# Two hybrid attention layers on one Trainium2 core: first logits, latent values, 1/sum and the start of the output projection in another order

## The reference, cut to what matters

```python
def hybrid_layer(x, ...):
    h = rms_norm(x, g_norm)
    z = jnp.einsum('bsd,dc->bsc', h, w_in)
    aq, ak, av, ag, bq, bk, bv, bg, cq, ckv, ckr, cg = jnp.split(z, idx, axis=-1)
    # A: 6 heads, keys and values shared by 3; rms norm, axial rope, full softmax
    oa = dense_gqa_blocks(qa, ka, va, HEAD_DIM ** -0.5) * jax.nn.silu(ag)
    # B: 6 heads, window of +-128 keys, a sink term in the sum
    ob = windowed_sink_gqa(qb, kb, vb, b_sink, HEAD_DIM ** -0.5) * jax.nn.silu(bg)
    # C: 4 heads, queries, keys and values out of latents cq and ckv
    qc = jnp.einsum('bsr,rc->bsc', rms_norm(cq, c_qn), c_wuq)
    kv = jnp.einsum('bsr,rc->bsc', rms_norm(ckv, c_kvn), c_wukv)
    oc = mla_blocks(qc_nope, qc_rope, kc_nope, kc_rope, vc, ...) * jax.nn.silu(cg)
    o = jnp.concatenate([oa, ob, oc], axis=-1)
    return x + jnp.einsum('bsm,md->bsd', o, w_out)
```

## Time and profile before

| | us |
|---|---|
| median of three executions | 1965.51 |
| lowest, highest | 1963.92, 1968.25 |
| the profiled execution: whole time | 1968.18 |
| the profiled execution: span of its instructions | 1966.4 |
| TensorE busy | 1878.5 (96%) |
| TensorE weight loads busy | 1489.7 (76%) |
| VectorE busy | 817.7 (42%) |
| ScalarE busy | 782.1 (40%) |
| GpSimd busy | 597.8 (30%) |

### The profile page before, as it was taken

How to read it: one execution, slowest core, us unless ns; L and a number is a source line. 1 busy time by engine, 2 the same in 40 slices (tenths; PEclk the granted TensorE clock), 3 DMA queues, 4 the chain that set the end, 5 groups by cost and what they waited for, 6 DMA issues and landing times.

```text
span 1966.4 us, 23067 instructions
## 1 busy us (share of the span) xinstructions
PE 1878.5 (96%) x9756; PEld 1489.7 (76%) x9756; DVE 817.7 (42%) x1338; ACT 782.1 (40%) x1286; POOL 597.8 (30%) x182
## 2 busy tenths in 40 slices
PE   8998899989999999999899999989998999998997
PEld 5777799988788888887788888877674468765456
DVE  7663545653123212102562035135635644625653
ACT  5974465443333333223332122224335533334541
POOL 3331432032232333444254434433420005322001
PEclk9998899989999999999899999989999999999999
DMA  5110000122323332232132323223110012211001
GB/s 198 65 65 0 1 1 21 45 91 75 135 96 107 97 112 85 87 107 86 45 127 86 107 86 107 86 86 137 67 65 22 1 43 99 86 63 44 1 1 43
DMA packets 28992, 141.54 MB, mean 72 GB/s; under 512 B 2871, under 2 KB 7351, under 8 KB 14936
## 3 DMA queue, kind: packets, MB, share of 16 engines
q1 hardware_dynamic: 18944, 122.94, 17.4%
q10 hardware_dynamic: 9944, 17.12, 2.6%
HBM read 134.80 MB, written 5.24 MB: 71 GB/s over the span
## 4 chain that ended last, share of the span: by engine, by line
PE 90%; DVE 4%; ACT 3%; POOL 2%; issue 1%; DMA 0%; POOLq 0%; SPq 0%; DVEq 0%; ACTq 0%
PE bank L403 54%; PE bank L1032 8%; PE bank L607 5%; PE bank L414 4%; PE bank L1977 3%; PE bank L1998 3%; PE bank L1984 2%; PE bank L1437 1%; ACT w_part L361 1%; PE bank L1413 1%; PE bank L655 1%; PE bank L1926 1%; PE bank L792 1%; ACT WK L2107 1%; PE bank L1068 1%
## 5 line engine op out<-in xcount | busy, mean ns | idle before, releaser
L403 PE MATMUL bank<-x_part,w_part 128*128 128x512 f32 x3264 | 764.8, 394 | 0.6 <-DVE x_part L571 0.6
L403 PEld LDWEIGHTS bank<-x_part,w_part 128*128 128x128 f32 x3264 | 614.6, 189 | 135.0 <-issue 6.1
L2424 POOL TENSOR_TENSOR w_part<-RAW,w_part 128x2048 fp32r<-128x2048 f32 (+1 forms) x90 | 402.9, 4480 | 819.4 <-ACT w_part L361 819.4
L2424 POOL TENSOR_TENSOR w_part<-WK,w_part 128x2048 fp32r<-128x2048 f32 (+1 forms) x30 | 125.1, 4169 | 376.7 <-ACT w_part L361 376.7
L361 ACT ACTIVATE w_part<-RAW 128x2048 fp32r<-128x2048 f32 (+1 forms) x90 | 166.5, 1851 | 175.7 <-PE bank L403 138.3
L403 PE MATMUL bank<-f_part,w_part 128*128 128x512 f32 x768 | 174.4, 389 | 0.0
L403 PEld LDWEIGHTS bank<-f_part,w_part 128*128 128x128 f32 x768 | 144.1, 188 | 29.9
L1032 PE MATMUL bank<-WK 128*128 128x128 f32 (+1 forms) x1056 | 125.0, 279 | 5.3 <-DVE WK L1265 3.7
L1032 PEld LDWEIGHTS bank<-WK 128*128 128x128 f32 (+1 forms) x1056 | 119.7, 194 | 7.6 <-DVE WK L1265 4.0
L1977 PE MATMUL bank<-WK 64*128 64x512 f32 (+3 forms) x256 | 81.7, 593 | 9.7 <-ACT STAT L2093 9.7
L903 DVE SCALAR_TENSOR_TENSOR WK<-bank,COL,WK 128x510 f32<-128x510 f32 (+1 forms) x96 | 71.6, 749 | 46.3 <-ACT WK L863 43.7
(11 more groups left out here) (281 smaller groups left out, 2392.8 us busy)
## 6 DMA issues: line engine op xcount, KB each, us to landing
RAW<-wts SPq DMA_DIRECT2D x84, 1024.0 KB, 4.8
WK<-wts SPq DMA_DIRECT2D x24, 1024.0 KB, 4.8
WK<-scratch ACTq DMA_DIRECT2D x16, 256.0 KB, 2.7
RAW<-wts SPq DMA_DIRECT2D x6, 512.0 KB, 3.4
WK<-wts SPq DMA_DIRECT2D x6, 512.0 KB, 3.5
scratch<-WK ACTq DMA_DIRECT2D x4, 768.0 KB, 3.3
WK<-xT SPq DMA_DIRECT2D x4, 512.0 KB, 5.8
WK<-xT ACTq DMA_DIRECT2D x1, 2048.0 KB, 12.7
```

The costliest lines, as they stand in the source:

```text
L403: mm = pe.eng.matmul(b[:, :], W[w][:, k, c:c + P], src[x][k], start=start and k == 0 and n == 0, stop=stop and k == kn - 1 and n == 2)
L2424: eng.tensor_tensor(low_part(i), raw_part(i), high_part(i).bitcast(F32), ALU.subtract).then_inc(w_split, 1)
```

## The change

In both layers:

- TensorE waits for `kready` (last key copy of ScalarE) and `qready` (last query rope of VectorE) instead of `ready` and `ready_act`. `gated` on VectorE now waits for its gate.
- Gates 0 to 3 get banks 0 to 3 in a pool of their own; the query rotations, gates 4 to 7 and the latent values get banks 4 to 7.
- The latent values (`uv`) are made in step 1 of the attention, and VectorE copies them instead of ScalarE.
- ScalarE's rounding for the last gate chunk moves from before the dummy Exp to step 6.
- GpSimd multiplies eight identities by the 1/sum columns of a head pair (`inverse_diagonal`), and TensorE spreads by two products of a block of ones with 512 columns of these scaled identities.
- `fm4` is cut in two functions; its banks come from the logits' pool, and k = 0 and 1 stand before the value products of the last head pair.

```diff
-        def fm(name, chunk, c0, src, bank=None, start=True, stop=True, need=None):
+        def fm(name, chunk, c0, src, bank=None, start=True, stop=True, need=None, pool=range(BANKS)):
...
-            b = bank if bank is not None else job(name)
+            b = bank if bank is not None else job(name, pool)
...
-        def fm4(names, chunk, src, need):
+        def fm4_banks(names, chunk, pool=range(BANKS)):
+            return [weights(chunk, c) for c in (0, 256)], [job(n, pool) for n in names]
+        def fm4_steps(names, halves, bs, src, need, ks):
             pe = q["pe"]
-            halves = [weights(chunk, c) for c in (0, 256)]
-            bs = [job(n) for n in names]
-            for k in range(len(src[0])):
+            for k in ks:
...
+        GATE_BANKS = (0, 1, 2, 3), (4, 5, 6, 7)
+        SPREAD = wk(35584, 2 * TT, P)
...
-                    fm((L, "G", j), f"L{l}G{g}", j % 4 * P, HTS)
+                    fm((L, "G", j), f"L{l}G{g}", j % 4 * P, HTS, pool=GATE_BANKS[g])
...
-            pe.wait_ge(*at((L, "ready")))
-            pe.wait_ge(*at((L, "ready_act")))
+            pe.wait_ge(*at((L, "kready")))
+            pe.wait_ge(*at((L, "qready")))
+            def late_values():
+                for t in range(TT):
+                    b = job((L, "uv", t), GATE_BANKS[1])
+                    E.matmul(b[:, 0:256], CL[:, 2, t * P:(t + 1) * P], UKV[:, 256:512], start=True, stop=True)...
...
-                pe.wait_ge(*at((L, "ri", m)))
-                for t in range(TT):
-                    for o in range(2):
-                        z = 80 + 4 * ((2 * m + o) % 4) + t
-                        mm = E.matmul(b[64 * o:64 * o + 64, t * P:(t + 1) * P], LST[:, z:z + 1].broadcast_to([P, 64]), ident, start=True, stop=True)
+                pe.wait_ge(*at((L, "ridiag", m)))
+                for o in range(2):
+                    mm = E.matmul(b[64 * o:64 * o + 64, :], ones[:, 0:64], SPREAD[:, TT * o:TT * o + TT, :], start=True, stop=True)
...
+                if i == 1:
+                    late_values()
+                if i == len(pairs) + 1:
+                    halves, bs = fm4_banks(outs, f"L{l}O0", LOGIT_BANKS)
+                    fm4_steps(outs, halves, bs, mixed, lambda k: (L, "mix", k), (0, 1))
...
-            fm4([(L, "O", i) for i in range(4)], f"L{l}O0", mixed, lambda k: (L, "mix", k))
+            fm4_steps(outs, halves, bs, mixed, lambda k: (L, "mix", k), range(2, KO))
             for i in range(4, KO):
                 fm((L, "O", i), f"L{l}O1", i % 4 * P, mixed)
...
-                    if j % 2:
+                    if j % 2 and j < KO - 1:
                         ahead(f"L{l}G{g}", (j - 1) % 4 * P)
...
+                if i == 6:
+                    ahead(f"L{l}G1", 2 * P)
...
+                if i == 1:
+                    for t in range(TT):
+                        dve.wait_ge(*at(("pe", (L, "uv", t))))
+                        V.tensor_copy(VT2[:, t, 256:512], ps((L, "uv", t))[:, 0:256])...
...
+            def inverse_diagonal(L, m):
+                pool.wait_ge(*at((L, "ri", m)))
+                if m:
+                    pool.wait_ge(*at(("pe", (L, "sp", m - 1))))
+                ri = LST[:, 80 + 8 * (m % 2):88 + 8 * (m % 2)]
+                eng.tensor_tensor(SPREAD, ident.unsqueeze(1).broadcast_to([P, 8, P]), ri.unsqueeze(2).broadcast_to([P, 8, P]), ALU.mult)...
```

42 lines of the change are left out of this document (27 added, 15 removed).

## The result

The changed kernel takes 1950.91 us (median of four executions, 1947.6 to 1951.27); the kernel before took 1965.29 in the same session (four, 1963.92 to 1968.25). The ratio is 0.9921, with a 95% interval of 0.9905 to 0.9938. The forecast was 1949.3, in a range of 1943 to 1956: right in sign, and 1.6 us off in size. The profiled execution spans 1949.1 us; the one of before spanned 1966.4.

What follows compares the result with a forecast made beforehand. TensorE, 90% of the span, was taken as the bound. Savings of 10.7 us in layer 0 and 11.1 in layer 1, less 5.6 lost, made 16.2 off the 1965.5 median: 1949.3 us, range 1943 to 1956.

Steps and rivals of the forecast that it cites:

- The bound: Whole kernel: TensorE is 90% of the span; changes off TensorE count only where TensorE waits for them.
- Part 1: Attention start, earliest logits: the 4.83 us idle goes, plus clock of 2.7 us in layer 1, 2.4 in layer 0.
- Part 2: Attention start, late latent values copied by VectorE: cost 0; without cover up to 2.8 us for a layer.
- Part 3: ScalarE's 1.90 us rounding moved to step 6, where it idles 2.11 us: cost 0, bound 1.9 us a layer.
- Part 4: Spread of 1/sum by scaled identities in the attention: cost 0, bound +-1.6 us; GpSimd's product hidden.
- Part 5: Attention end, output projection begun before the last values: saves 3.6 us in layer 1, 3.5 in layer 0.
- The banks: Layer 1's output 4 lands in bank 3, waits for output 3's residual addition: 3.5 us plus 2.1 clock, 5.6 lost.
- The sum: Both layers: 10.7 saved in layer 0, 11.1 saved and 5.6 lost in layer 1; 16.2 us less, from the median.
- (a): Output 4 of layer 1: the bank costs less, 2 to 5.6 us better, 1943.7 to 1947; chance 0.12.
- (b): Attention start: a new wait for first probabilities cuts the gain by 3 to 4 us a layer, 1955 to 1957; chance 0.12.
- (c): Attention loop: GpSimd's diagonals hold VectorE, up to 47 us on top, 1996, slower than before; chance 0.03.
- (d): Attention loop: the gap moves into longer waits for ScalarE, half the start gain back, 1956; chance 0.05.

Runs made afterwards that it cites:

- The start alone: Kernel before with only the earliest logits, late latent values and moved rounding: 1949.03 us against 1965.74, ratio 0.9915.

## Why the prediction was right, and where its sizes were off

**The bound.** Right: the chain is TensorE's to 90% before and after, and what the change does on other engines moved nothing.

**Part 1.** Right. Predicted 7.5 us for layer 1 and 7.2 for layer 0; by the stages 7.7 and 7.4. The first probability was forecast at T + 2.9 and stands at T + 2.8, the first turn at T + 6.9 and stands at T + 6.7. The start alone shows that this part carries the change: 16.7 us of the medians in that session, 1.6 more than the 15.1 of the two starts by the stages; in its profiled execution the clock also stayed high behind the holes at the end.

**Part 2.** Right at 0: the copies take 0.39 us each, for which the bound was 0.69, and TensorE waits for none.

**Part 3.** Right at 0 for its new place: GpSimd's low part of that chunk (1797.35 to 1801.88) lies behind the first diagonal and ahead of the second, as said. What it gives at its old place I had not priced by itself; the run with the rounding back shows 0.5 us a layer.

**Part 4.** Right at 0: TensorE's spread takes 1.03 us, where 1.04 stood before, and undoing it changed nothing. The diagonal takes 1.90 us and not the 2.39 of the nearest row; that row has an operand and a result of other kinds. The hold of VectorE's residual splits that the prediction named ("up to 2.4 us") is there with 1.2 us, and hidden.

**Part 5.** The mechanism was right: idle 2.24 to 0.25 (I had said 0.2), values at 2.80 (2.9). The size, 3.6 and 3.5 us, was met in the pair of profiled executions, 3.7 and 3.6. But 1.6 to 1.7 us of each is a clock price that not every execution pays: the same hole left in place cost it in six of twelve cases. Part of it may belong to Part 1, if the new start makes that price rarer; this is not shown. Counted without it, this part gives 2.0 us a layer.

**The banks.** The step that reading the order gave, and the diff doesn't say, was right in its place, its layer, its releaser and its length: 3.46 us of idle, 3.5 predicted with the shift of the start. Predicted with the clock 5.6, found 5.2 (3.62 + 1.58); the bounds of the clock part, 0 to 2.8, held the five cases (1.55 to 2.92) but for 0.1.

**The sum.** Predicted 16.2, in the pair of profiled executions 17.2, of the medians 14.4. The term that fails is not one of a part but the step "I take the difference from the median": the difference was worked out from one execution of before that lay 2.9 us above its median, and took its lower clocks for the kernel's. That the forecast still came within 1.6 us is in part luck: the stages gave 1.0 us more than the sum, against the 2.9 that were counted too much. Against the second execution of before the same stages give 6.76 + 8.35 (starts) + 1.98 + 3.67 (ends) - 5.20 = 15.56; taking off 0.26 behind the last landmark and 0.50 ahead of the first leaves 14.8, the difference of the spans (1963.9 - 1949.1), close to the 14.4 of the medians. The 2.5 us between the two spans of before are the joint product (0.9), the first logits (0.7 less in layer 0, 0.6 more in layer 1) and the values of layer 0 (1.6).

**The rivals.** (a) did not come in this size: the bank cost 5.2 of the 5.6. Mended, it is worth 5.0. (b): no new wait at the start, and the run with the rounding back shows that even 1.8 us more on ScalarE would have cost only 0.5 a layer. (c) falls by the doubled diagonals; its mechanism exists, at one hidden place. (d) falls: seven waits in the loop, 5.2 us, as before.

## What to carry to other kernels

When a group of jobs leaves a rotation of banks, walk the rotation on to the next borders and name the last tenant of each bank there; here one such border took back 5 us of 22, and one argument gave them back. Split the price of an idle time into the idle, which every execution pays, and the lower clock behind it, which some don't; take the second from more than one execution before it is booked to a change. And a wait that appears just ahead of others for the same engine's work may cost nothing: compare to the next landmark, not the idle itself.

## What the runs showed of the hardware that I had not expected

The clock behind one and the same idle differs between executions of one kernel: behind 2.24 us the twelve records took 2.80 us or 4.36 in the kernel before, in the same layer. The Trainium skill, TensorE: Matmul & The Clock Gate, "What's actually happening", says of the start of a kernel that the number of products that run slow there changes from run to run of the same kernel; behind these holes within a kernel it does too, and behind the one of 2.24 us it was none at all in six of twelve cases.

A GpSimd product over 128 x 1024 with both factors broadcast took 1.90 us, sixteen times to 0.01, where one over tensors of that size without broadcasting took 2.39. Which of the two operands or the type of the result makes the difference was not tried.
